# A two-layer hybrid diffusion step on one Trainium2 core: the first latent step opened beside the context top-k, its expert rows spread evenly, w_out by tiles

## The chip, the cores and the metric

The kernel is one program on one core of a Trainium2 chip. The metric is the time of one execution on the device in microseconds; before the change three runs gave a median of 3172.74 us. All data are float32.

## The reference, cut to what matters

There are two layers. In each, a context sequence of 128 tokens and a latent sequence of 256 tokens go through the same weights; the latent one also reads cached context keys and states. D is 1024. PEER retrieves 128 expert rows of U and 128 of V for each token.

```python
def trunk_layer(x, cond, lp, layer_idx, ctx_k, ctx_v, init_f, init_b, latent):
    sh1, sc1, g1, sh2, sc2, g2 = adaln(cond, lp["mod_w"], lp["mod_b"])
    mix, k, v, s_f, s_b = token_mixers(modulate(x, lp["norm1_w"], sh1, sc1), lp, ...)   # w_in, three mixers, w_out
    x = x + g1 * mix
    x = x + g2 * peer_ffn(modulate(x, lp["norm2_w"], sh2, sc2), lp)

def peer_ffn(h, lp):
    q = (xt @ lp["peer_wq"]).reshape(n_tok, 8, 2, 128)
    s = jnp.einsum("thmd,mhnd->thmn", q, lp["peer_keys"])
    v1, i1 = lax.top_k(s[:, :, 0], 16); v2, i2 = lax.top_k(s[:, :, 1], 16)
    top_s, pos = lax.top_k(v1[..., :, None] + v2[..., None, :], 16)      # flattened to 256
    g = jax.nn.softmax(top_s)
    act = jnp.einsum("td,thkd->thk", xb, u_tab[ib])
    return jnp.einsum("thk,thkd->td", jax.nn.gelu(act) * gb, v_tab[ib])
```

## The kernel before

The work is four steps: step 0 is the context of layer 0, step 1 the latent of layer 0, steps 2 and 3 the same of layer 1. A context step has T = 1 tile of 128 tokens, a latent one T = 2. Each step has a dense part (`dense`, one generator for each engine) and a gather, which fetches the picked rows. The gather of a step runs beside the dense part of the next step, and that of step 3 by itself at the end.

**The dense part.** ACT squares x and DVE modulates (`square`, `modulate`, with `inverse_rms` at L1076, a Newton iteration in small VectorE instructions); PE transposes the result (`turn_h`) and multiplies it by w_in in six chunks, q, k, v, xb1, xb0, pz (L606, L616). Then come rope, convolution, the state scan, eight attention heads for a latent step, w_out (L801), transposed keys (L809), the second modulation, the query projection by wq in four chunks (L819), the scores (L831) and, for each tile, `choose`: the top-k on DVE (L1138, L1141, L1146 and what follows), which ends with the mark "picked" (L1246). ACT copies out of PSUM (L889) and takes the softmax exponent in between. The arrays of a step live in regions of one buffer `work`; q and k of a step lie at 0 to 2047, and so do the two one-hot arrays `hot` of the top-k.

**Weights.** SP loads them in chunks of 2 MB into a ring of two (`wring`, `load_chunk` at L359). A chunk is issued when the chunk two before it has been used. SP's order is written out by hand from L456: the chunks, between them the modulation rows (`modulation`, `store_row`, L398, which waits until ACT or DVE has taken the row from PSUM), the modulation vectors, the cached keys, the bands and so on. The last two modulation rows of a layer, 10 and 11, are loaded behind wq of the context step and taken by ACT at its very end.

**The gather.** POOL issues one indirect DMA for each row index of all 128 tokens (L552): 128 partitions of 4 KB, 512 KB. There are 768 such rows of U and 768 of V. They land in a ring of 10 buffers `rows`; from the gather of step 3 on, the 8 halves of `wring` serve too, 18 in all. A buffer is refilled when its row was used, in a fixed order (L547). DVE takes the dot product of a U row with h (L1520), ACT the gelu of 64 of them, DVE multiplies by the gates and spreads the weights of 16 rows (`share`, L1506), and PE accumulates V rows in PSUM in groups of four (L858). When all 128 V rows of a tile are in, DVE adds the sum to x (L1543).

**What sets the order.** Each engine's program is one fixed list. `dense` yields a name at each pause ("start", ("in", 0) ... "mid", ("wq", i), ("ps", t), ("choose", t, i), ("exp", t)), and `run_beside` (L1699) puts there the gather events that the plan has for this name: "u" or "v" (four rows), "g" (gelu), "w" (gates), "s" (share), "x" (sum). `pauses_of` (L1582) gives every pause a weight and `spread` (L1655) hands out the events by weight. `events_one` (L1610) orders the events of a context step's gather in four groups: the first 64 U rows, the first 64 V rows, the other 64 U, the other 64 V, and in `gather_plans` (L1666) each group belongs to one stretch of the latent step: start to dt, ("in", 5) to wo, mid to ("wq", 3), ("ps", 0) to ("exp", 0). `events_two` (L1629) orders those of a latent step's gather evenly: V rows follow 19 groups (LAG) behind U rows. Its first 8 groups of U (EARLY) go beside the second top-k of the step itself, 80% (ROOM) of the rest beside the next context step, and what is left comes after that step (`plan[None]`).

**w_out and what follows.** PE multiplies by w_out column half by column half, both tiles in each half; DVE multiplies by the gate and adds to x (L1483 to L1488); then comes the pause "mid", and after its events DVE modulates (L1490).

## Time and profile before

| | us |
|---|---|
| Median of three runs | 3172.74 |
| Lowest, highest | 3164.27, 3186.46 |
| The profiled execution, its own time | 3179.57 |
| Its span in the profile | 3177.8 |
| Busy in the span: PE, DVE, POOL, ACT | 1557.0, 1617.2, 1734.1, 239.0 |
| First "picked", first row issue | 336.0 |
| Bytes moved by DMA | 981.71 MB |

The windows view gives for stretches of the span the busy time and number of instructions of each engine, TensorE's granted clock as a share of full speed, the busy share of the 16 DMA engines and the rate. POOL's instruction count in a stretch is the number of rows issued. The timeline view gives start and length of instructions, and in brackets how long the engine stood idle before them and what released it. "Issue" is idle time without a releaser.

### The profile page before, as it was taken

Reading aid. Unit: us, or ns where it says so; the run is one execution under the profiler, and the core shown is the slowest. Engines: PE = TensorE matmul, PEld = TensorE weight load, DVE = VectorE, ACT = ScalarE, POOL = GpSimd, SP = SyncE. Lnnn points to the kernel's source line nnn. Section 1 sums busy time; section 2 is a strip of 40 time slices with the busy share of each in tenths; the row PEclk is TensorE's granted clock in tenths of the full one; section 3 lists DMA queues with packets and bytes.
Section 4 is the critical chain, followed back from the end, with each engine's and each line's share of the span. In section 5 each row is a group of like instructions: output and inputs, shape, how many; then the busy total and the mean of one; then the engine's idle time right before and its main releaser. Section 6 shows DMA issues by size and latency. Waiting matters only on the chain.

```text
span 3177.8 us, 22396 instructions
## 1 busy us (share of the span) xinstructions
PE 1557.0 (49%) x6699; PEld 676.8 (21%) x6699; DVE 1617.2 (51%) x4301; ACT 239.0 (8%) x551; POOL 1734.1 (55%) x1540
## 2 busy tenths in 40 slices
PE   6776476756522456645225577666530033332354
PEld 1424253344100132113001144225300000000011
DVE  0124784377397444443861076447639844445411
ACT  0211112111000001000000012110000000000000
POOL 0000663366647655555775673447554867676764
PEclk8888688778666767767557787787765565555576
DMA  6553796778968998999999988678785899999998
GB/s 221 190 193 122 293 399 244 262 259 341 343 204 337 385 342 321 361 368 393 342 331 360 361 326 331 248 263 322 287 331 165 273 376 357 367 368 360 343 361 306
DMA packets 310468, 981.71 MB, mean 309 GB/s; under 512 B 29774, under 2 KB 36212, under 8 KB 310092
## 3 DMA queue, kind: packets, MB, share of 16 engines
q0 software_dynamic: 221184, 805.40, 68.2%
q1 hardware_dynamic: 89164, 174.88, 15.2%
q8 instruction: 54, 0.88, 0.1%
q14 instruction: 66, 0.54, 0.0%
HBM read 976.93 MB, written 3.24 MB: 308 GB/s over the span
## 4 chain that ended last, share of the span: by engine, by line
DVE 23%; PE 22%; issue 18%; DMA 17%; POOL 13%; another core or an unknown queue 5%; ACT 2%; SPq 0%; POOLq 0%; DVEq 0%; ACTq 0%
POOL rows L552 10%; DMA rows<-peer_v_in,vidx 8%; PE acc L858 8%; DVE rows L1520 7%; DMA rows<-peer_u_in,idx 4%; PE psum L574 4%; POOL wring L552 3%; PE psum L801 3%; PE psum L819 2%; DVE work L1141 2%; DVE work L1138 1%; DVE wring L1520 1%; DMA wring<-peer_v_in,vidx 1%; DVE work L1344 1%
## 5 line engine op out<-in xcount | busy, mean ns | idle before, releaser
L552 POOL DMA_INDIRECT rows<-peer_u_in,idx x650 | 793.5, 1221 | 731.2 <-DVE gates L1244 335.6
L1520 DVE CUSTOM_DVE_ANT_0 rows<-rows,hn 128x1024 f32<-128x1024 f32 x650 | 780.0, 1224 | 462.2 <-DMA rows<-peer_u_in,idx 425.1
L552 POOL DMA_INDIRECT rows<-peer_v_in,vidx x654 | 689.6, 1054 | 576.2 <-PE acc L858 349.1
L858 PE MATMUL acc<-rows,vw 128*32 128x512 f32 x2616 | 535.4, 910 | 869.8 <-DMA rows<-peer_v_in,vidx 758.1
L858 PEld LDWEIGHTS acc<-rows,vw 128*32 128x32 f32 x2616 | 107.4, 144 | 1225.1 <-issue 1185.6
L574 PE MATMUL psum<-wring,cond 128*2 128x512 f32 x384 | 186.1, 641 | 112.4 <-DMA wring<-mod_w_in 112.4
L858 PE MATMUL acc<-wring,vw 128*32 128x512 f32 x456 | 128.6, 988 | 192.1 <-DMA wring<-peer_v_in,vidx 92.1
L606 PE MATMUL psum<-wring,work 128*128 128x512 f32 (+1 forms) x480 | 193.0, 559 | 19.6 <-DMA wring<-w_in_in 10.0
L1520 DVE CUSTOM_DVE_ANT_0 wring<-wring,hn 128x1024 f32<-128x1024 f32 x118 | 142.0, 1223 | 113.5 <-DMA wring<-peer_u_in,idx 105.3
L819 PE MATMUL psum<-work,wring 128*128 128x128 f32 (+1 forms) x1024 | 182.1, 342 | 20.1 <-DMA wring<-peer_wq_in 17.4
L889 ACT ACTIVATE work<-psum 128x512 f32<-128x512 f32 (+3 forms) x256 | 110.9, 451 | 908.2 <-PE psum L606 183.7
L552 POOL DMA_INDIRECT wring<-peer_u_in,idx x118 | 136.3, 1155 | 67.8 <-issue 34.4
L819 PEld LDWEIGHTS psum<-work,wring 128*128 128x128 f32 x1024 | 163.2, 201 | 42.5 <-issue 22.9
L552 POOL DMA_INDIRECT wring<-peer_v_in,vidx x114 | 114.5, 1004 | 49.2 <-issue 32.0
L1506 DVE TENSOR_TENSOR vw<-const,wv 128x512 f32<-128x512 f32 x48 | 33.0, 690 | 206.0 <-PE acc L858 140.3
L606 PEld LDWEIGHTS psum<-wring,work 128*128 128x128 f32 x480 | 90.2, 207 | 124.1 <-issue 108.3
L594 PE MATMUL psum<-const,hn 128*128 128x128 f32 x96 | 22.7, 415 | 144.0 <-DVE hn L1132 140.4
L1543 DVE TENSOR_TENSOR acc<-acc,mod_g 128x512 f32<-128x512 f32 x12 | 7.8, 692 | 166.9 <-PE acc L858 121.8
L574 PEld LDWEIGHTS psum<-wring,cond 128*2 128x2 f32 x384 | 33.0, 90 | 258.5 <-issue 255.0
L801 PE MATMUL psum<-wring,work 128*128 128x512 f32 x192 | 86.7, 613 | 0.8 <-ACT work L1025 0.8
L616 PE MATMUL psum<-work,wring 128*128 128x128 f32 (+1 forms) x384 | 76.8, 368 | 16.1 <-DMA wring<-w_in_in 16.1
L858 PEld LDWEIGHTS acc<-wring,vw 128*32 128x32 f32 x456 | 24.8, 152 | 274.2 <-issue 244.9
(203 smaller groups left out, 1394.2 us busy)
## 6 DMA issues: line engine op xcount, KB each, us to landing
wring<-mod_w_in SPq DMA_DIRECT2D x24, 2048.0 KB
wring<-w_in_in SPq DMA_DIRECT2D x20, 2048.0 KB
wring<-peer_wq_in SPq DMA_DIRECT2D x16, 2048.0 KB
wring<-w_out_in SPq DMA_DIRECT2D x8, 2048.0 KB
rows<-peer_v_in,vidx POOLq DMA_INDIRECT x654
rows<-peer_u_in,idx POOLq DMA_INDIRECT x650
wring<-w_in_in SPq DMA_DIRECT2D x4, 1056.0 KB
mod_a<-mod_scratch SPq DMA_DIRECT2D x8, 512.0 KB
```

The source lines that it names most:

```text
L552: nc.gpsimd.indirect_dma_start(slots[slot_of[n]], None, table, bass.IndirectOffsetOnAxis(ap=at[:, col + r:col + r + 1], axis=0))\
L574: mm(p[0:2, :], cond3[:, b, :], w[:, b, :], start=(b == 0), stop=False)
L606: ins = mm(p[:, 0:n], hT[0][:, b, t * P:(t + 1) * P], w[:, b, slot:slot + n], start=(b == 0), stop=(b == DB - 1))
L616: ins = mm(p[:, 0:st.N], w[:, b, i * P:(i + 1) * P], hT[0][:, b, 0:st.N], start=(b == 0), stop=(b == DB - 1))
L801: ins = mm(p[:, :], catT[:, b, t * P:(t + 1) * P], chunk("wo", k, cc)[:, b, :], start=(b == 0), stop=(b == DB - 1))
L819: ins = mm(p[:, 0:N], chunk("wq", k, b // 4)[:, kb, (b % 4) * P:(b % 4 + 1) * P], hT[1][:, kb, 0:N], start=(kb == 0), stop=(kb == DB - 1))
L858: ins = mm(acc[half][QUAD * j:QUAD * (j + 1), :], w[:, at:at + QUAD], four[j][0][:, half * CHUNK:(half + 1) * CHUNK], start=(r == 0), stop ...
L889: A(dst, src, ACT.Copy, scale=scale).then_inc(*take(*key))
L1138: d(V.max(top[:, b * TOPK + 8 * r:b * TOPK + 8 * r + 8], values[:, b * width:(b + 1) * width]))
L1141: d(V.max_index(index[:, b * TOPK + 8 * r:b * TOPK + 8 * r + 8], top[:, b * TOPK + 8 * r:b * TOPK + 8 * r + 8], values[:, b * width:(b + 1 ...
L1506: V.tensor_tensor(vw[q % 2][:, :].rearrange("p (g t) -> p g t", t=QUAD), c("quad").unsqueeze(1).broadcast_to(wide), wv[:, q * SHARE:(q + 1 ...
L1520: V.tensor_tensor_reduce(held, held, hn[n][:, :], 1.0, 0.0, ALU.mult, ALU.add, dots[:, col + r:col + r + 1]).then_inc(u_used, 1)
```

## The change

- The first part of `dense` becomes a generator `opening`: the first square and modulation, the transposes and the q and k projections. For step 1 alone (`early`) it runs inside step 0, at the pauses that `BEFORE` names: after ("wq", 1), ("wq", 2) and ("ps", 0). Its two chunks are loaded behind step 0's wq and ahead of modulation rows 10 and 11. `hot` of the context steps moves to 4096 to 8191.
- The gather of step 0, beside step 1, is ordered by `events_two` and spread over the whole step from ("in", 2) to ("exp", 1). In step 3 the four groups stay, but the last is spread to ("exp", 1).
- PE multiplies by w_out tile by tile; "mid" becomes one pause for each tile, and each tile is squared and modulated ahead of its pause. The transposes of all tiles but the last come ahead of those of the keys. The weights of the pauses change.
- `inverse_rms` does three iterations of two instructions (three for four columns) and one scaling, where it did four of three (four).
- The rows left over after step 2 get 12 more buffers in `work`, those after step 3 get 17. POOL waits for the last "picked" of the step before the first of them. A row takes the free buffer that was used longest ago.
- SP loads the cached keys and values behind pz and waits for the "picked" of the step before.
- In `events_one` the share event stands one place later.

```diff
-        hot = [region(0, 2048), region(2048, 2048)]
+        hot = {False: [region(0, 2048), region(2048, 2048)], True: [region(4096, 2048), region(6144, 2048)]}
...
-            chunks += [(("q", k), ("q", k, last)), (("k", k), ("k", k, last)), (("v", k), ("v", k, last)),
+            if not st.early:
+                chunks += [(("q", k), ("q", k, last)), (("k", k), ("k", k, last))]
+            chunks += [(("v", k), ("v", k, last)),
                        (("xb1", k), ("xb", k, 5)), (("xb0", k), ("xb", k, 3)), (("pz", k), ("pz", k, last))]
             if st.first:
...
+            if k + 1 < STEPS and steps[k + 1].early:
+                chunks += [((name, k + 1), (name, k + 1, steps[k + 1].T - 1)) for name in "qk"]
...
+        left_free = [region(2560 + i * D, D) for i in range(12)]
+        spare(left_free, after_step[STEPS - 2], row_no["u", STEPS - 2, 0, 0])
+        spare([wring[i][:, j * D:(j + 1) * D] for i in range(W_SLOTS) for j in range(DB * CHUNK // D)],
+              row_no["u", STEPS - 1, 0, 0], len(stream))
+        spare([region(i * D, D) for i in range(17)], after_step[STEPS - 1], len(stream))
+        slot_of, held_before, filled, last_in = [], {}, {}, {}
+        for n in range(len(stream)):
+            free = list(range(RING)) + [i for which, first, last in extra if first <= n < last for i in which]
+            slot = min(free, key=lambda i: last_in.get(i, -1))
+            slot_of.append(slot)
             held_before[n] = last_in.get(slot)
             last_in[slot] = n
             filled[n] = filled.get(held_before[n], 0) + 1
+
+        left_by = {after_step[STEPS - 2]: ("picked", STEPS - 2, 0),
+                   after_step[STEPS - 1]: ("picked", STEPS - 1, 1)}
...
+                if st.lat:
+
+                    sp.wait_ge(*after("picked", k - 1, steps[k - 1].T - 1))
+                    sp.wait_ge(*after("h1", k, st.T - 1))
+                    load(k_cached, io["cache_attn_k"][0, layer].rearrange("n h d -> n (h d)"), "cache_in", layer)
+                    load(v_cached, io["cache_attn_v"][0, layer].rearrange("n h d -> n (h d)"), "cache_in", layer)
...
+                if k + 1 < STEPS and steps[k + 1].early:
+                    load_chunk("q", k + 1)
+                    load_chunk("k", k + 1)
...
+                if n in left_by:
+                    pool.wait_ge(*after(*left_by[n]))
...
-                for cc in range(2):
-                    pe.wait_ge(*chunk_landed("wo", k, cc))
-                    for t in range(T):
+                for t in range(T):
+                    for cc in range(2):
+                        pe.wait_ge(*chunk_landed("wo", k, cc))
                         p = job(pe, "wo", k, t, cc)
                         for b in range(DB):
                             ins = mm(p[:, :], catT[:, b, t * P:(t + 1) * P], chunk("wo", k, cc)[:, b, :],
                                      start=(b == 0), stop=(b == DB - 1))
                         ins.then_inc(*made("wo", k, t, cc))
+                    yield ("mid", t)
+                for t in range(T - 1):
+                    turn_h(st, 1, t)
                 pe.wait_ge(*after("keys_in", k))
                 for i in range(4):
                     p = job(pe, "kt", k, i)
...
                         b = 4 * i + j
                         ins = tr(p[:, j * P:(j + 1) * P], keys_nat[:, b * P:(b + 1) * P], ident)
                     ins.then_inc(*made("kt", k, i))
-                yield "mid"
-                turn_h(st, 1)
+                turn_h(st, 1, T - 1)
...
-                for _ in range(4):
+
+                scale = 1.0
+                for _ in range(3):
                     if w == 1:
                         d(V.scalar_tensor_tensor(by, out, mean, out, ALU.mult, ALU.mult))
                     else:
...
                         settle()
                         d(V.tensor_tensor(by, by, mean, ALU.mult))
                     settle()
-                    d(V.tensor_scalar(by, by, -0.5, 1.5, ALU.mult, ALU.add))
-                    settle()
-                    d(V.tensor_tensor(out, out, by, ALU.mult))
-                    settle()
+                    d(V.scalar_tensor_tensor(out, by, 3.0 * scale * scale, out, ALU.subtract, ALU.mult))
+                    settle()
+                    scale *= -2.0 * scale * scale
+                d(V.tensor_scalar(out, out, 1.0 / scale, None, ALU.mult))
...
+            def opening(st):
+                yield "start"
+                modulate(st, 0)
+                yield "h"
+                yield ("in", 0)
+                yield ("in", 1)
...
-                for cc in range(2):
-                    for t in range(T):
-                        tmp = mixed if (cc * T + t) % 2 == 0 else xw
+                for t in range(T):
+                    for cc in range(2):
+                        tmp = mixed if cc == 0 else xw
...
-                yield "mid"
-                modulate(st, 1)
+                    modulate(st, 1, t)
+                    yield ("mid", t)
...
-    names += [("start", 0)]
-    names += [(("in", i), w * T) for i, w in enumerate((15, 7, 7))]
-    names += [("rope", 0)]
+    if not st.early:
+        names += [("start", 0), ("h", 5 * T)]
+        names += [(("in", i), w * T) for i, w in enumerate((10, 7))]
+    names += [(("in", 2), 7 * T), ("rope", 0)]
     names += [(("in", i), w * T) for i, w in ((3, 4.5), (4, 7))]
     names += [("dt", 4), (("in", 5), 7 * T), ("conv", 7), ("xw", 9)]
     for t in range(T):
         names += [(("decay", t), 3), (("seg", t), 14)]
     names += [("y", 3)]
     names += [(("head", i), 6) for i in range(T * ATT_HEADS)]
-    names += [("wo", 9), ("mid", 15 * T)]
-    names += [(("wq", i), (15 if i == 0 else 7) * T) for i in range(4)]
+    names += [("wo", 9)]
+    names += [(("mid", t), 14 if t == 0 else 10) for t in range(T)]
+    names += [(("wq", i), (10 if i == 0 else 7) * T) for i in range(4)]
...
-            groups = left
-            spread(plan, part("start", "dt"), groups[0])
-            spread(plan, part(("in", 5), "wo"), groups[1])
-            spread(plan, part("mid", ("wq", 3)), groups[2])
-            spread(plan, part(("ps", 0), ("exp", 0)), groups[3])
+            if steps[k].early:
+
+                spread(plan, part(("in", 2), ("exp", 1)), left)
+            else:
+                groups = left
+                spread(plan, part("start", "dt"), groups[0])
+                spread(plan, part(("in", 5), "wo"), groups[1])
+                spread(plan, part(("mid", 0), ("wq", 3)), groups[2])
+                spread(plan, part(("ps", 0), ("exp", 1)), groups[3])
...
-            left = events_one(steps[k])
+            left = events_two(steps[k]) if steps[k + 1].early else events_one(steps[k])
...
+BEFORE = {("wq", 1): ("start",), ("wq", 2): ("h",), ("ps", 0): (("in", 0), ("in", 1))}
...
+    def work(st):
+        following = steps[st.k + 1] if st.k + 1 < len(steps) else None
+        ahead = opening(following) if following and following.early else None
+        if st.first:
+            for name in modulation(st.layer):
+                if st.k:
+                    yield name
+        if not st.early:
+            yield from opening(st)
+        for name in dense(st):
+            yield name
+            for expected in BEFORE.get(name, ()) if ahead else ():
+                assert next(ahead) == expected
+        if ahead:
+            assert next(ahead, None) is None
```

## Rows read from the trace of the kernel before

**Rows 1.** The page: busy shares and slices of the span.
```profile
PE 1557.0 (49%) x6699; PEld 676.8 (21%) x6699; DVE 1617.2 (51%) x4301; ACT 239.0 (8%) x551; POOL 1734.1 (55%) x1540
...
DMA  6553796778968998999999988678785899999998
```

**Rows 2.** Windows by stage: from:to, length, each engine's busy us, PE's clock, DMA share, GB/s.
```profile
282.50:336.00 53.50, 15.33 (x36) 2.55 (x33) 50.09 (x246) 1.05 (x3) 0.00 (x0) 0.68 0.05 18
336.00:460.00 124.00, 90.78 (x272) 52.71 (x272) 95.96 (x177) 13.30 (x27) 95.45 (x72) 0.83 1.01 391
460.00:610.00 150.00, 89.05 (x499) 45.89 (x499) 70.98 (x230) 36.13 (x92) 56.17 (x59) 0.75 0.74 270
610.00:686.00 76.00, 38.26 (x129) 18.13 (x128) 41.34 (x87) 6.87 (x13) 36.27 (x29) 0.72 0.71 249
686.00:766.00 80.00, 65.94 (x313) 57.49 (x314) 52.86 (x96) 10.54 (x24) 66.90 (x44) 0.93 0.95 354
766.00:881.00 115.00, 57.71 (x280) 13.22 (x280) 60.16 (x275) 3.10 (x6) 64.86 (x65) 0.69 0.87 316
881.00:968.00 87.00, 9.62 (x22) 1.44 (x20) 85.14 (x298) 0.31 (x1) 42.65 (x30) 0.57 0.55 177
1515.00:1640.00 125.00, 29.22 (x132) 5.66 (x136) 97.44 (x315) 0.42 (x1) 92.69 (x79) 0.56 0.94 341
1650.00:1835.00 185.00, 94.27 (x444) 20.29 (x444) 30.57 (x79) 5.91 (x10) 109.70 (x112) 0.71 0.95 351
2099.00:2246.00 147.00, 98.72 (x383) 72.83 (x380) 93.19 (x177) 15.23 (x33) 92.42 (x71) 0.81 0.86 312
2246.00:2462.00 216.00, 56.00 (x296) 14.48 (x294) 145.11 (x584) 6.40 (x10) 109.58 (x98) 0.59 0.69 246
2462.00:2502.00 40.00, 0.00 (x0) 0.00 (x0) 38.55 (x67) 0.00 (x0) 33.90 (x21) 0.50 0.79 256
2541.00:3165.00 624.00, 224.35 (x1020) 46.61 (x1024) 241.38 (x440) 0.77 (x3) 430.26 (x427) 0.60 0.95 361
2550.00:2575.00 25.00, 7.43 (x36) 1.53 (x40) 10.84 (x19) 0.00 (x0) 18.98 (x20) 0.64 1.03 411
```

**Rows 3.** POOL's waits in step 1, 336 to 968 us: total, times, longest.
```profile
POOL rows L552 <- PE acc L858: 108.1, 19, 32.1
...
POOL rows L552 <- DVE dots L1520: 73.3, 9, 22.3
```

**Rows 4.** POOL's waits in the last gather, 2541 to 3165 us.
```profile
POOL rows L552 <- remote: 38.3, 13, 4.9
...
POOL rows L552 <- DVE dots L1520: 5.9, 1, 5.9
```

**Rows 5.** Timeline of SP's queue at the start of step 1.
```profile
338.33 1.49 SPq L372 DMA_DIRECT2D wring<-w_in_in  x2
```

**Rows 6.** Timeline of PE in step 1: start, length, what, idle before it.
```profile
358.87 29.99 PE L606 MATMUL psum<-wring,work 128*128 128x512 f32 x64 [7.59 <-issue]
394.49 19.00 PE L606 MATMUL psum<-wring,work 128*128 128x512 f32 x64 [5.63 <-DMA wring<-w_in_in]
...
614.85 27.73 PE L801 MATMUL psum<-wring,work 128*128 128x512 f32 x64
...
678.18 1.97 PE L594 MATMUL psum<-const,hn 128*128 128x128 f32 x8 [33.85 <-DVE hn L1132]
```

**Rows 7.** Timeline of DVE: steps 0, 1 and 3, three gaps.
```profile
282.79 3.19 DVE L1138 MAX8 work<-work 128x8 f32<-128x128 f32 x16 [41.77 <-ACT work L889]
...
875.09 1.30 DVE L1543 TENSOR_TENSOR acc<-acc,mod_g 128x512 f32<-128x512 f32 x2 [31.42 <-PE acc L858]
...
2369.80 1.30 DVE L1543 TENSOR_TENSOR acc<-acc,mod_g 128x512 f32<-128x512 f32 x2 [45.10 <-remote]
```

**Rows 8.** The page: costliest groups, busy and mean ns of one.
```profile
L1520 DVE CUSTOM_DVE_ANT_0 rows<-rows,hn 128x1024 f32<-128x1024 f32 x650 | 780.0, 1224 | 462.2 <-DMA rows<-peer_u_in,idx 425.1
```

**Rows 9.** One line of the inverse root: duration ns min, median, max.
```profile
L1095 DVE TENSOR_SCALAR root<-root x108: 153/154/286, 49.0 to 3173.0; 128x1 f32<-128x1 f32 x84, 128x4 f32<-128x4 f32 x24
```

More of the change, by code:

```diff
@@ L861, in gather @@
                             ins.then_inc(v_used, 1)
-            run_beside(steps, plans, lambda layer: modulation(layer, MOD_ORDER[:4]), dense, gather)
+            run_beside(steps, plans, lambda layer: modulation(layer, MOD_ORDER[:4]), opening, dense, gather)
         @block.scalar
@@ L889, in carry, with square @@
                 A(dst, src, ACT.Copy, scale=scale).then_inc(*take(*key))
-            def square(st, which):
-                for t in range(st.T):
+            def square(st, which, only=None):
+                for t in range(st.T) if only is None else (only,):
                     if which == 0:
@@ L1059, in _ @@
             A(cond[:, :], bank("cond")[:, 0:16], ACT.Silu).then_inc(*take("cond"))
-            run_beside(steps, plans, modulation, dense, gather)
+            run_beside(steps, plans, modulation, opening, dense, gather)
         @block.vector
@@ L1567, in _ @@
             dve.wait_ge(*after("consts_in"))
-            run_beside(steps, plans, modulation, dense, gather)
+            run_beside(steps, plans, modulation, opening, dense, gather)
     assert sorted(map(str, took)) == sorted(map(str, numbers)), "each psum job is taken once"
@@ L1620, in events_one @@
         for n, v in enumerate(vs):
[L1621 removed]
+            if n % share == 3 and share < n < lot - share:
                 line.append(("s", k, 0, first + n // share + 1))
@@ L1708, in run_beside @@
         if k < len(steps):
[L1709 removed]
             seen = []
[L1711 to L1716 removed]
+            for name in work(steps[k]):
                 seen.append(name)
                 beside(name)
[L1719 removed]
+            assert seen == [n for n, _ in pauses_of(steps[k])], seen
         beside(None)
```

95 lines of the change are left out of this document (47 added, 48 removed).

## The prediction

> **What bounds the kernel now.** I read the page's shares and slices first, then the windows by stage, then POOL's waits, then single gaps of PE and DVE. No engine is full over the span: PE 49%, DVE 51%, POOL 55%, while the slices of DMA stand at 8 or 9 in most places and dip to 6 or less in a few [rows 1]. Below, "step 0" to "step 3" are context and latent of layer 0, then of layer 1; the rows gathered by POOL (1536 of 512 KB, 805 MB) are most of the traffic. Undisturbed, POOL issues 20 rows in 25 us, 1.25 us each, at 411 GB/s [rows 2]. Against this the stages differ. Step 1 lasts from 336 to 968 us (632 us), and only its first 124 us run at 391 GB/s; then come 270, 249, 354, 316 and 177 GB/s [rows 2]. In this step POOL stood 108.1 us for a buffer that PE had not freed and 73.3 us for one that DVE had not [rows 3]: 181 us of 632. So step 1 is bound by the ring of 10 buffers: its consumers sit in a fixed order behind dense work. The same holds of step 3 (312 GB/s in 2099 to 2246, 246 in 2246 to 2462). The last gather, 2541 to 3165, is different: 361 GB/s, DMA share 0.95, and POOL waits there 38.3 us for a remote party but only 5.9 us for DVE [rows 2, 4]. That stage is bound by transfer. Beside step 0's top-k (282.5 to 336) DMA is idle, share 0.05 [rows 2]. That is where the opening goes.
>
> **The opening of step 1 beside step 0's top-k.** Before, after the pick at 336: w_in's q and k chunks are issued at 338.33 [rows 5], PE multiplies both from 358.87 for 29.99 us, then waits 5.63 us for v, which starts at 394.49 [rows 6]. Afterwards v and xb1 stand in the place of q and k. I expect their issue at 338 as before, since SP still waits at the store of modulation row 10, which ACT takes behind the top-k. So v starts near 359, not 394.5: 35 us off the start of step 1, whose section to 460 becomes 89 us instead of 124. It then holds 10 of the 32 U groups (40 rows) where 72 were issued [rows 2]. Cost in step 0: DVE's two modulations, behind whose wait for mod_a the whole top-k is queued, lie in its 41.77 us gap before it [rows 7]; mod_a is issued between the wq chunks, as now. PE's 30 us of q and k start behind the scores, with 53.5 us to hide in, and ACT's eight copies with them. The two 2 MB chunks take idle DMA. If this cover failed, the pick would come up to 35 us later and nothing were won. Upper bound of the loss: 35; taken: 0.
>
> **U and V evenly through step 1.** The new plan has 77 events over weights of 397, from v's projection to the last piece of the second top-k. I count per section:
> - 460 to 610 (convolution, scan, heads): 13 groups of U and 3 of V, before 59 rows issued, nearly all V. DVE gets 52 rows at 1.224 us [rows 8], 64 us more on top of 71 busy of 150 [rows 2]; PE loses some ten groups of V, 3.5 us each (224.35 us for 1020 matmuls in the last gather, 16 to a group of four rows [rows 2]). Ends: +64 if every U row lies on the chain, -35 if only the V rows did. DVE waits in this part for others in more than half of the time, so I take +14, giving 164.
> - 610 to 686 (w_out to the turned h2): below, 42 instead of 76.
> - 686 to 766 (queries): PE is busy 66 of 80 [rows 2] and gets five V groups more, 18 us, while U rows go; +3 taken (0 to +18), giving 83.
> - 766 to 968 (two top-k): before 65 + 30 issues in 202 us [rows 2], with DVE standing 31.42 us for the last V before tile 0's sum [rows 7]. Now 40 rows in the first top-k and 48 + 32 in the second: 120. The nearest row is step 2's top-k, where U and V already alternate: 79 issues in 125 us, 1.58 us each [rows 2]. 120 x 1.58 = 190, so -12. Ends: 1.31 us, a row at 400 GB/s (157), and 2.9 us (348).
> Sum: 89 + 164 + 42 + 83 + 190 = 568 against 632, **-64 us**.
>
> **w_out by tiles, and "mid".** Before, PE sits idle 33.85 us for h2 behind the keys [rows 6], since DVE takes five U groups between x_mid and the modulation. Now each tile is modulated straight after its x_mid and U follows. w_out (27.73 us [rows 6]), one modulation (15 small instructions of 0.2 us and two passes about as long as a U row, 5 us), and some 9 for transposes and copies make 42 for the 76 us: -34 in step 1, counted above. In step 3 it is the same gap, but behind it the wq chunks and 44 rows load. 2099 to 2246 took 147 us for 71 rows and 8 MB at 312 GB/s [rows 2]; at 390 it would be 118. I take 122: **-25** (-10 to -34).
>
> **The two top-k of step 3.** The old plan spends all 64 V rows of tile 0's second lot up to "exp 0", and DVE stands 45.10 us before the sum [rows 7]; in 2246 to 2462 it is busy 145 of 216 [rows 2]. The new plan stretches them to "exp 1". 64 V + 32 U = 96 rows at 1.58 are 152 us; DVE's 145 plus small waits is the longer: 166. **-50** (-15 to -60).
>
> **The rest.** inverse_rms loses 5 instructions of 15, about 0.2 us each [rows 9], on 27 calls: 27 us of DVE, of which I count 4 in step 0, where nothing covers it, and 5 in step 2 with its reordered square; elsewhere it is inside the sections. The reordered keys cost nothing: PE transposes them while DVE modulates, as now. SP's new wait for the earlier pick holds the cached keys, and behind them the band, the states and w_out, but that pick is done at 336 and the loads come after pz, still ahead of their users: 0 (to +5). The share event moved from 2 to 3 belongs to a plan that step 0's rows no longer use: 0 to 2.
> Late slots: 12 more buffers for the rows left over after step 2 (1650 to 1835, 112 issues, 351 GB/s, share 0.95 [rows 2]) are worth at most the missing 5% plus the hand-over; against them stands POOL's new wait for the pick, which all later issues queue behind. **-5** (-20 to +10). 17 more in the last gather free POOL from 5.9 us of DVE [rows 4], not from the remote waits. But POOL now waits there for the second pick. Before it had run 18 rows ahead, worth 18 x 1.28 = 23 us (512 KB at 411 GB/s), of which part was lost again, since after the pick DVE's rows back to back held POOL to 21 issues in 40 us [rows 2]. **+10** (-15 to +23).
>
> **Sum**: -4 - 64 - 5 - 5 - 25 - 50 + 10 = -143. The profiled execution took 3179.6 us (span 3177.8), so 3036.6; it lay 7 above the median of 3172.7, so **3030 us**. A change under 1% could not be told from none.
>
> **The rivals.**
> (a) *POOL is held by DVE.* In 2462 to 2502 DVE is busy 38.55 of 40 and POOL needs 33.90 / 21 = 1.61 us an issue instead of 0.95, 1.90 with the gap [rows 2]. If the top-k does this to rows too, step 1's 120 cost 228 (+38) and step 3's 96 cost 182 (+16): **3084**. Against it: 1.58 in step 2. The Trainium skill (SBUF — State Buffer, "Who interferes with whom") has it that a VectorE instruction with two SBUF inputs contends only with GpSimd's reads, and that descriptor writing should not suffer. The U rows have two SBUF inputs, and the trace disagrees: 1.61 against 0.95 us.
> (b) *The top-k runs at the free pace.* If most of its instructions leave POOL alone and the slots are enough, 120 rows cost 1.31 us, 157: 33 less, and the tail's +10 becomes -10: **2977**. For it: DVE's busy work there is only 145 us. Against it: no top-k in the trace ran so. By the same section, an instruction with one SBUF input leaves GpSimd alone, which would favour this rival.
> (c) *The top-k stretches stay as they are*, because PE's V groups and DVE's shares wait for each other whatever the order: only the other gains, 81 us, remain: **3092**.
> (d) *Slower.* With V rows for two top-k in one ring of 10, U rows of the new tile queue behind V rows whose weights DVE makes only between its pieces, and the 881 to 968 pace (30 rows in 87 us, 2.9 us) holds for all 216 rows of the four top-k: 626 us against 418. +208 - 81 gives **3300**. It decides from (418 + 81) / 216 = 2.31 us per row. For it: that is the pace of the stage that mixes the two now. Against it: there DVE had 52 us of top-k and all of 32 U rows, and few rows were planned.
> That the opening doesn't leave step 1 would show as 3065 and is part of (a)'s neighbourhood.
>
> **How the numbers follow.** Forecast 0.58, (a) 0.15, (c) 0.12, (b) 0.09, (d) 0.06. The range takes in (b), (a) and (c) with their slack: 2970 to 3115; outside are (d) and the far edges. Slower by over 1% is (d), 0.06; within 1% (3141 to 3204) are the worst of (a) and (c) together, 0.06; faster 0.88.
>
> **What would show it.** First U issue still at 334 to 338 and v's product at about 359. Step 1 over near 900 to 905, its POOL waits under 120 us, PE's gap before h2 under 10 us. DVE's wait before the sum in step 3 gone or under 10. The last gather as long as before or slightly longer. The forecast is wrong if the first pick moves, if the sections 460 to 610 grow beyond 190 us, or if rows in the top-k cost over 2 us.

## The result, and the profile after

The changed kernel takes 3072.23 us (3069.44 to 3083.75, four runs) against 3170.34 us for the kernel before (four runs as well): a ratio of 0.969 with a 95% interval of 0.9646 to 0.9734, 3.1% faster. The profiled execution took 3070.95 us, span 3069.2, so 108.6 us less than the one of before. The forecast was 3030 with a range of 2970 to 3115: right in kind and within the range, too large in the gain (143 us against 108.6 in the profiled executions and 98.1 in the medians).

The page of the changed kernel: DMA's slices stand at 8 or 9 from the ninth to the 25th, where the old page had a 6 in the twelfth, step 1's second top-k [rows 1]. They still dip in the seventh and eighth slice, the scan and heads of step 1, and in most from the 26th to the 31st, in step 3.

```profile
PE 1617.9 (53%) x6699; PEld 688.4 (22%) x6699; DVE 1595.5 (52%) x4160; ACT 240.0 (8%) x552; POOL 1724.9 (56%) x1540
...
DMA  6555796699999999999899989669697999999997
```

For a comparison by stages I cut both spans at the same five kinds of instruction: the gates of a step's last pick, the first matmul of w_out, the first of the queries, the first MAX8 of the top-k, and DVE's sum. The windows of the changed kernel (columns as in [rows 2]):

```profile
332.00:593.70 261.70, 129.25 (x528) 79.73 (x528) 185.86 (x414) 44.83 (x109) 150.22 (x114) 0.70 0.80 292
593.70:633.40 39.70, 36.22 (x133) 16.64 (x129) 20.44 (x43) 6.31 (x12) 21.76 (x20) 0.97 0.81 292
633.40:718.00 84.60, 75.68 (x377) 58.10 (x378) 28.62 (x49) 8.65 (x21) 39.45 (x39) 0.90 0.94 356
718.00:904.20 186.20, 80.87 (x374) 17.86 (x373) 145.74 (x575) 5.39 (x9) 129.75 (x117) 0.61 0.93 333
904.20:1628.60 724.40, 337.12 (x1471) 127.51 (x1470) 389.98 (x929) 49.16 (x114) 453.61 (x388) 0.70 0.95 353
1628.60:1772.20 143.60, 88.42 (x396) 19.31 (x394) 6.66 (x22) 2.58 (x5) 92.36 (x98) 0.76 0.99 387
1772.20:2040.50 268.30, 186.49 (x801) 102.07 (x801) 163.96 (x378) 49.70 (x117) 143.26 (x125) 0.81 0.82 305
2040.50:2082.20 41.70, 33.08 (x101) 16.45 (x97) 25.77 (x53) 6.42 (x12) 18.38 (x16) 0.89 0.76 283
2082.20:2177.70 95.50, 67.48 (x297) 58.53 (x298) 65.16 (x108) 10.17 (x23) 69.20 (x56) 0.82 0.97 371
2177.70:2347.20 169.50, 56.51 (x282) 13.12 (x280) 139.98 (x568) 5.15 (x8) 97.96 (x86) 0.58 0.76 267
2347.20:3058.40 711.20, 271.24 (x1024) 59.21 (x1024) 313.85 (x578) 1.02 (x4) 508.74 (x480) 0.60 0.94 356
```

Set beside the kernel before, cut the same way:

| Stage | before | after | difference | forecast |
|---|---|---|---|---|
| up to step 0's pick | 334.8 | 332.0 | -2.7 | -4 |
| step 1: pick to w_out | 280.1 | 261.7 | -18.4 | -21 |
| step 1: w_out to queries | 71.5 | 39.7 | -31.8 | -34 |
| step 1: queries to top-k | 80.5 | 84.6 | +4.1 | +3 |
| step 1: two top-k | 194.6 | 186.2 | -8.4 | -12 |
| step 2 | 714.5 | 724.4 | +9.9 | -5 |
| left-over rows of step 2 | 148.6 | 143.6 | -5.0 | -5 |
| step 3: to w_out | 274.5 | 268.3 | -6.2 | 0 |
| step 3: w_out to top-k | 148.8 | 137.2 | -11.6 | -25 |
| step 3: two top-k | 214.4 | 169.5 | -44.9 | -50 |
| the last gather | 703.7 | 711.2 | +7.5 | +10 |

The opening: PE multiplies by q and k from 281.94, beside the top-k; SP issues the next chunks at 335.60, behind the stores of the modulation rows; v starts at 356.44, and PE has stood 30.30 us for it. First PE's timeline, then SP's, of the changed kernel:

```profile
281.94 27.73 PE L638 MATMUL psum<-wring,work 128*128 128x512 f32 x64 [0.90 <-ACT work L927]
...
356.44 19.04 PE L638 MATMUL psum<-wring,work 128*128 128x512 f32 x64 [30.30 <-DMA wring<-w_in_in]
```

```profile
332.09 2.14 SPq L426 DMA_DIRECT2D mod_scratch<-mod_rows  x2
...
335.60 47.28 SPq L397 DMA_DIRECT2D wring<-w_in_in  x4
```

The wait before a tile's sum is gone. In step 3 DVE goes from the last U row straight to the gates and the sum, where [rows 7] had 45.10 us (timeline of DVE, changed kernel):

```profile
2345.46 1.22 DVE L1572 CUSTOM_DVE_ANT_0 rows<-rows,hn 128x1024 f32<-128x1024 f32 x1
...
2347.16 0.29 DVE L1292 TENSOR_TENSOR gates<-work,small 128x128 f32<-128x128 f32 x1
2347.49 1.30 DVE L1595 TENSOR_TENSOR acc<-acc,mod_g 128x512 f32<-128x512 f32 x2
```

POOL's waits in step 1 fell from 181 us [rows 3] to 148, which is more than the 120 that the prediction gave as a sign of being right:

```profile
POOL rows L584 <- PE acc L896: 92.5, 21, 13.7
...
POOL rows L584 <- DVE dots L1572: 55.5, 10, 19.3
```

### The profile page after: what moved, and what is told of

It reads as the page before. It is cut to its first block, busy times and chain, and to the rows that moved or that the text cites. A ratio compares the mean times of both kernels' runs of the same rounds, so it can differ in the third digit from the quotient of the medians.

```text
span 3069.2 us, 22265 instructions
## 1 busy us (share of the span) xinstructions
PE 1617.9 (53%) x6699; PEld 688.4 (22%) x6699; DVE 1595.5 (52%) x4160; ACT 240.0 (8%) x552; POOL 1724.9 (56%) x1540
## 4 chain that ended last, share of the span: by engine, by line
PE 28%; issue 20%; DVE 19%; DMA 17%; POOL 11%; another core or an unknown queue 3%; ACT 2%; SPq 0%; POOLq 0%; DVEq 0%; ACTq 0%
PE acc L896 10%; DVE rows L1572 6%; POOL rows L584 5%; DMA rows<-peer_v_in,vidx 5%; DMA rows<-peer_u_in,idx 5%; POOL work L584 4%; PE psum L857 4%; PE psum L606 4%; DMA wring<-w_in_in 3%; PE psum L638 2%; PE psum L837 2%; POOL wring L584 2%; DMA work<-peer_v_in,vidx 2%; DVE work L1189 1%
## 5 line engine op out<-in xcount | busy, mean ns | idle before, releaser
L584 POOL DMA_INDIRECT rows<-peer_u_in,idx x591 | 710.3, 1202 | 651.0 <-DVE gates L1292 332.8
L1572 DVE CUSTOM_DVE_ANT_0 rows<-rows,hn 128x1024 f32<-128x1024 f32 x591 | 708.2, 1224 | 436.3 <-DMA rows<-peer_u_in,idx 410.2
L584 POOL DMA_INDIRECT rows<-peer_v_in,vidx x519 | 567.0, 1092 | 485.1 <-PE acc L896 306.1
L896 PE MATMUL acc<-rows,vw 128*32 128x512 f32 x2076 | 434.0, 901 | 592.1 <-DMA rows<-peer_v_in,vidx 454.0
L896 PE MATMUL acc<-work,vw 128*32 128x512 f32 x720 | 216.8, 855 | 331.5 <-DMA work<-peer_v_in,vidx 179.5
L584 POOL DMA_INDIRECT work<-peer_v_in,vidx x180 | 183.5, 1019 | 92.4 <-issue 50.1
L857 PE MATMUL psum<-work,wring 128*128 128x128 f32 (+1 forms) x1024 | 183.6, 343 | 11.6 <-DMA wring<-peer_wq_in 8.6
L1572 DVE CUSTOM_DVE_ANT_0 work<-work,hn 128x1024 f32<-128x1024 f32 x110 | 133.1, 1224 | 102.7 <-DMA work<-peer_u_in,idx 84.6
L584 POOL DMA_INDIRECT work<-peer_u_in,idx x110 | 120.9, 1099 | 48.3 <-issue 32.9
L584 POOL DMA_INDIRECT wring<-peer_u_in,idx x67 | 69.6, 1039 | 23.8 <-issue 22.0
```

Source lines behind the costliest of these rows:

```text
L584: nc.gpsimd.indirect_dma_start(slots[slot_of[n]], None, table, bass.IndirectOffsetOnAxis(ap=at[:, col + r:col + r + 1], axis=0))\
L857: ins = mm(p[:, 0:N], chunk("wq", k, b // 4)[:, kb, (b % 4) * P:(b % 4 + 1) * P], hT[1][:, kb, 0:N], start=(kb == 0), stop=(kb == DB - 1))
L896: ins = mm(acc[half][QUAD * j:QUAD * (j + 1), :], w[:, at:at + QUAD], four[j][0][:, half * CHUNK:(half + 1) * CHUNK], start=(r == 0), stop ...
L1572: V.tensor_tensor_reduce(held, held, hn[n][:, :], 1.0, 0.0, ALU.mult, ALU.add, dots[:, col + r:col + r + 1]).then_inc(u_used, 1)
```

## The experiments

Three sets were run, each on a chip of its own and with the kernel before beside it. The kernel before took 3156.82, 3055.34 and 3173.49 us in them, so times of different sets aren't compared; ratios to the kernel before are. The bases are 0.969 (with the result) and 0.9696 (set 2). From the two intervals, a difference between two ratios is known to 0.5 or 0.6%, 15 to 19 us.

Stages differ between the sets as well. In set 1 the kernel with "exp 0" in step 3 has the same step 1 as the changed kernel, and its step 1 takes 580.6 us, not the 572.2 of the profile with the result. It is the base for step 1 in that set. Its four stretches (pick to w_out, to the queries, to the top-k, to the pick):

```profile
333.00:601.70 268.70, 134.56 (x529) 83.17 (x529) 185.50 (x413) 44.77 (x109) 150.62 (x114) 0.68 0.79 285
601.70:641.30 39.60, 36.15 (x132) 16.60 (x128) 20.41 (x43) 6.30 (x12) 21.72 (x20) 0.97 0.82 292
641.30:726.00 84.70, 75.68 (x377) 58.09 (x378) 28.64 (x49) 8.67 (x21) 39.78 (x39) 0.90 0.94 356
726.00:913.60 187.60, 79.13 (x377) 18.07 (x376) 145.53 (x576) 5.35 (x9) 129.65 (x117) 0.66 0.92 331
```

### Set 1: one part taken out

**The opening put back.**

```diff
-                self.early = k == 1
+                self.early = False
+                self.even = k == 1
...
-            if steps[k].early:
-
-                spread(plan, part(("in", 2), ("exp", 1)), left)
+            if steps[k].even:
+
+                spread(plan, part("start", ("exp", 1)), left)
```

> The changed kernel with the opening of step 1 put back at the start of step 1; its rows still alternate, now spread from "start" to the second "exp". My theory (each stage bound by the ring pays for itself): the pick of step 0 stays at 332 to 335 us, step 1 grows by 25 to 35 us, and the whole is 3095 to 3107. Rival (the rows only move, and transfer gives the time back later): at most 10 us more, 3072 to 3082.

Measured: 3086.46 us, ratio 0.9794 (0.9753 to 0.9835), so 1.0% above the base, 33 us. Step 1 takes 594.9 us, 14.3 more than in the base of its set (22.7 more than with the result):

```profile
335.00:627.20 292.20, 168.49 (x640) 97.60 (x640) 205.81 (x453) 50.28 (x120) 167.58 (x130) 0.73 0.82 305
627.20:666.90 39.70, 36.21 (x133) 16.70 (x129) 16.60 (x36) 6.30 (x12) 12.07 (x12) 0.97 0.76 265
666.90:763.70 96.80, 75.59 (x361) 58.09 (x362) 27.56 (x47) 10.04 (x23) 49.07 (x44) 0.85 0.88 320
763.70:929.90 166.20, 71.30 (x358) 16.77 (x357) 140.75 (x568) 3.88 (x7) 112.51 (x103) 0.67 0.91 325
```

Up to w_out it is 23.5 us longer than in its set's base and up to the top-k 12 more, but the two top-k take 166.2 instead of 187.6, with 14 fewer rows left for them. With the even order the opening pays; part of it is given back. The rival (at most 10 us) is out by the ratio, if narrowly. Where the rest of the 33 us lies isn't shown: the profiled execution was one of the two quickest of this kernel (3079.9 us).

**The four groups kept.**

```diff
-            if steps[k].early:
-
-                spread(plan, part(("in", 2), ("exp", 1)), left)
-            else:
+            if True:
                 groups = left
-                spread(plan, part("start", "dt"), groups[0])
+                spread(plan, part(("in", 2) if steps[k].early else "start", "dt"), groups[0])
...
-            left = events_two(steps[k]) if steps[k + 1].early else events_one(steps[k])
+            left = events_one(steps[k])
```

> The changed kernel with the early opening, but step 0's rows in the four old groups (64 U, 64 V, 64 U, 64 V) over the stretches in 2 to dt, in 5 to wo, mid to wq 3, ps 0 to exp 1. My theory: the first stretch becomes bound by transfer (64 rows and four chunks in some 90 us) and eats most of what the opening saves, so 20 to 35 us more, 3092 to 3107. Rival (the order doesn't matter once the last group reaches exp 1): within 8 us of 3072.

Measured: 3072.82 us, ratio 0.9733 (0.9678 to 0.9788), 0.4% above the base, within what can be told. Step 1 takes 572.9 us: as long as with the result, and 7.7 less than in the base of its set.

```profile
333.90:425.00 91.10, 59.64 (x192) 38.65 (x192) 62.60 (x101) 4.53 (x12) 69.76 (x51) 0.75 0.98 369
333.90:609.90 276.00, 155.79 (x720) 87.00 (x720) 153.57 (x352) 43.13 (x108) 153.90 (x131) 0.72 0.83 308
609.90:651.60 41.70, 32.76 (x100) 16.29 (x96) 25.74 (x53) 6.42 (x12) 18.46 (x17) 0.92 0.77 281
651.60:748.00 96.40, 66.60 (x311) 57.79 (x312) 65.09 (x108) 9.71 (x23) 79.64 (x56) 0.84 0.99 373
748.00:906.80 158.80, 59.04 (x276) 13.45 (x276) 140.24 (x568) 3.89 (x7) 101.99 (x88) 0.61 0.84 301
```

The first part of the mechanism is as I expected: the first stretch is full at 369 GB/s, w_out comes 7 us later than in the set's base, and the queries take 12 us more. But I priced it wrongly: the top-k, with 88 rows instead of 117, gives back 29 us. My forecast of 20 to 35 us fell, and the rival's "within 8 us" holds of step 1 in the profiles.

**Step 3's last group to exp 0 again.**

```diff
-                spread(plan, part(("ps", 0), ("exp", 1)), groups[3])
+                spread(plan, part(("ps", 0), ("exp", 0)), groups[3])
```

> The changed kernel, but in step 3 the last 64 V rows and the sum end at exp 0 again, as before the change. My theory: DVE's wait of about 45 us before the sum comes back, the two top-k of step 3 take 205 to 215 us instead of 169.5, and the whole is 3105 to 3117. Rival (rows moved out of the stretch are found again in the last gather): 3075 to 3090.

Measured: 3110.81 us, ratio 0.9865 (0.9822 to 0.9908), 1.75% or some 55 us above the base; in the profiles 32.5 us of span, of two sets. DVE waits again (timeline), and the two top-k take 203.7 us:

```profile
2288.98 1.30 DVE L1595 TENSOR_TENSOR acc<-acc,mod_g 128x512 f32<-128x512 f32 x2 [34.47 <-remote]
```

```profile
2179.80:2383.50 203.70, 53.78 (x269) 12.55 (x268) 142.86 (x571) 5.12 (x8) 91.29 (x86) 0.58 0.63 229
```

It is the same 86 rows and about the same busy time of DVE (143 us) as in 169.5 us; the other three kernels of this set, with "exp 1", take 165.6 to 167.4. What a better order of this stretch saves is not given back later: the last gather takes 707.4 us here and 706 to 712 in those three.

**The old order of w_out and mid** (the shown core is DVE's; PE and ACT likewise).

```diff
-                for t in range(T):
-                    for cc in range(2):
-                        tmp = mixed if cc == 0 else xw
+                for cc in range(2):
+                    for t in range(T):
+                        tmp = mixed if (cc * T + t) % 2 == 0 else xw
...
-                    modulate(st, 1, t)
-                    yield ("mid", t)
+                for t in range(T):
+                    yield ("mid", t)
+                modulate(st, 1)
```

> The changed kernel with w_out by column halves for both tiles, the keys ahead of both transposes, and U rows ahead of both modulations again. My theory: w_out to the queries takes 70 us instead of 40 in steps 1 and 3; in step 1 this is paid in full, in step 3 by 12 us, together 3105 to 3117. Rival (the queries are bound by transfer in both steps and take back what is lost): 3080 to 3092.

Measured: 3101.45 us, ratio 0.9831 (0.98 to 0.9862), 1.4% above the base; 25.5 us of span. W_out to the queries takes 58.8 and 60.9 us instead of 39.7 and 41.7 (not 70, most likely because the new weights give "mid" fewer rows: 24 are issued where it was 29). In step 3 the queries then take 83.9 us instead of 95.5 with the result, or 93 to 94 in this set:

```profile
601.50:660.30 58.80, 39.67 (x133) 18.53 (x129) 26.15 (x52) 6.52 (x12) 25.16 (x24) 0.79 0.79 284
660.30:743.40 83.10, 74.07 (x377) 57.00 (x378) 22.77 (x39) 8.64 (x21) 33.82 (x36) 0.91 0.80 300
2066.10:2127.00 60.90, 33.40 (x101) 17.01 (x97) 35.12 (x69) 6.52 (x12) 31.85 (x24) 0.76 0.76 259
2127.00:2210.90 83.90, 69.53 (x311) 60.05 (x312) 55.34 (x92) 9.83 (x23) 64.69 (x49) 0.87 0.98 370
```

In step 3, where the queries run at 370 GB/s, 19 us saved ahead of them cost 9 to 12 in them. In step 1 they run at 300 here and give next to nothing back (83.1 us against 84.7); over the whole of step 1 13.5 us are left.

### Set 2: late buffers, v earlier, the even order in step 3

**The base.**

> The changed kernel itself, as the base for its neighbours on this chip: ratio to the kernel before 0.965 to 0.973 as measured with the result.

Measured: 2965.59 us, ratio 0.9696 (0.966 to 0.9732).

**Without the late buffers.**

```diff
-        spare(left_free, after_step[STEPS - 2], row_no["u", STEPS - 2, 0, 0])
...
-        spare([region(i * D, D) for i in range(17)], after_step[STEPS - 1], len(stream))
...
-                if n in left_by:
-                    pool.wait_ge(*after(*left_by[n]))
```

> The changed kernel without the 12 and the 17 late buffers and without POOL's two new waits for the pick (the 8 buffers in wring stay). My theory: the 12 are worth about 5 us between step 2's pick and the last sum of its left-over rows, the wait before the last gather costs about as much, so within 10 us of the changed kernel either way. Rival (the deeper ring carries the gain): 20 to 40 us slower.

Measured: 2971.8 us, ratio 0.973 (0.9694 to 0.9766), 6 us beside the base and not to be told from it. The left-over rows take 144.8 instead of 140.0 us, as sized, and the last gather 646.6 instead of 649.3, so that of the +10 for POOL's wait no more than 3 are seen here. The rival is out.

**v and xb1 ahead of the stores.**

```diff
                              .broadcast_to([2, CHUNK]), "nw_in", layer, j)
+                    if j == order[-1]:
+                        for key in ahead:
+                            load_chunk(*key)
                     if j != order[0]:
                         store_row(*before)
...
-                    modulation(layer, MOD_ORDER[10:])
+                    modulation(layer, MOD_ORDER[10:], [("v", k + 1), ("xb1", k + 1)] if steps[k + 1].early else ())
```

> The changed kernel with the v and xb1 chunks of step 1 issued ahead of the stores of modulation rows 10 and 11, so beside step 0's top-k. In the profile of the changed kernel PE stands 30.3 us for v at the start of step 1. My theory: v is multiplied before the pick, the convolution starts 20 to 25 us earlier, and 8 to 20 us remain at the end of step 1, since DMA is then the bound of the first stretch: 0.3 to 0.6% faster than the changed kernel. Rival (the stretch is bound by DVE's and the ring's order): no gain, within 5 us.

Measured: 2947.33 us, ratio 0.9627 (0.9579 to 0.9674), 18 us or 0.6% under the base of its set. Its four runs took 2933.95 to 2959.38 us, those of the base 2959.12 to 2969.12, but the intervals of the two ratios overlap: faster than the changed kernel in all likelihood. The product of v starts at 329.2, before the pick at 335.0 (timeline of PE):

```profile
329.20 17.47 PE L642 MATMUL psum<-wring,work 128*128 128x512 f32 x64
346.52 7.15 PE L652 MATMUL psum<-work,wring 128*128 128x256 f32 x32
362.48 15.68 PE L652 MATMUL psum<-work,wring 128*128 128x256 f32 x64 [8.80 <-DMA wring<-w_in_in]
```

The pick to w_out takes 247.8 instead of 264.6 us. Of these 17 us, 12 are left at the end of step 1, which takes 559.2 us against 571.5 (571.1 and 568.9 in the two other kernels of this set, whose step 1 is that of the base).

**The even order beside step 3 too.**

```diff
-            else:
-                groups = left
-                spread(plan, part("start", "dt"), groups[0])
-                spread(plan, part(("in", 5), "wo"), groups[1])
-                spread(plan, part(("mid", 0), ("wq", 3)), groups[2])
-                spread(plan, part(("ps", 0), ("exp", 1)), groups[3])
+            spread(plan, part(("in", 2) if steps[k].early else "start", ("exp", 1)), left)
...
-            left = events_two(steps[k]) if steps[k + 1].early else events_one(steps[k])
+            left = events_two(steps[k])
```

> The changed kernel with step 2's rows alternating evenly over the whole of step 3 as well, from start to the second exp. My theory: the scan and heads of step 3 take more rows (125 issues now in 268 us), the queries fewer, and POOL's waits of 72.7 us for PE before w_out halve; step 3 gets 10 to 30 us shorter, 3045 to 3063 where the changed kernel takes 3072. Rival (the order within the step is nothing, as the pair with four groups in step 1 suggests): within 8 us.

Measured: 3007.36 us, ratio 0.9835 (0.9796 to 0.9874), 1.4% slower than the base: my theory fell, and the rival too. Step 3 takes 574.1 us instead of 536.3. The stretch up to w_out, of the base and then of this kernel:

```profile
1769.00:2028.40 259.40, 181.29 (x800) 98.20 (x800) 163.58 (x378) 49.94 (x117) 137.66 (x122) 0.81 0.84 317
```

```profile
1765.80:2049.80 284.00, 171.14 (x640) 99.49 (x640) 206.34 (x455) 49.88 (x117) 153.32 (x121) 0.74 0.79 289
```

POOL issues the same number of rows, 122 and 121, but DVE is busy 206 us instead of 164: it takes 106 U rows in this stretch instead of 66, between the small steps of scan and heads. POOL's wait moves from PE (71.5 to 36.6 us) to DVE (18.2 to 55.4 us):

```profile
POOL rows L584 <- DVE dots L1572: 55.4, 5, 16.4
POOL rows L584 <- PE acc L896: 36.6, 4, 11.5
```

### Set 3: what each part gives by itself

**Four iterations** of the old loop in the changed kernel.

```diff
-                for _ in range(3):
+                for _ in range(4):
...
-                    d(V.scalar_tensor_tensor(out, by, 3.0 * scale * scale, out, ALU.subtract, ALU.mult))
+                    d(V.tensor_scalar(by, by, -0.5, 1.5, ALU.mult, ALU.add))
+                    settle()
+                    d(V.tensor_tensor(out, out, by, ALU.mult))
...
-                d(V.tensor_scalar(out, out, 1.0 / scale, None, ALU.mult))
```

> The changed kernel with four iterations of the old form in inverse_rms (135 more small VectorE instructions of 0.2 us). My theory: the calls in step 0, and a few behind SSD and heads, lie on the path; 4 to 12 us slower than the changed kernel, ratio to the kernel before 0.970 to 0.974. Rival (all hidden under transfers): 0.967 to 0.970.

Measured: 3093.46 us, ratio 0.9733 (0.9703 to 0.9764), 0.4% above the base, 13 us, and inside the ratios expected; 22.5 us of span, of two sets. That is no more than the two ratios can differ by chance, and this set has no run of the changed kernel, so neither my 4 to 12 us nor the rival is ruled out.

**Four groups and the early v**, the two edits shown above together.

```diff
+                spread(plan, part(("in", 2) if steps[k].early else "start", "dt"), groups[0])
...
+                        for key in ahead:
+                            load_chunk(*key)
```

> Step 0's rows in the four groups and v and xb1 ahead of the stores. With the even order the early v brought the ratio from 0.9696 to 0.9627. My theory: in the groups the first stretch holds 64 U rows and is bound by transfer, so that nothing of the early v is left, ratio 0.969 to 0.975. Rival (the gain is one of PE's chain, whatever the order): 0.962 to 0.967.

Measured: 3079.77 us, ratio 0.9701 (0.9672 to 0.973). The groups without the early v had 0.9733, and the two intervals overlap. The early v gives 17 us up to w_out in the even order and nothing here: 277.2 us against 276.0. The products of w_in end 58 us after the pick instead of 91, but the first matmul of dt starts 123 us after it instead of 122, as DVE has 60 U rows ahead of the steps that it needs. PE stands idle for 65 us (timeline; in the groups without the early v it is 30.60). The profile names nobody for this wait; in the opening-alone kernel below, where it is 28.75, it names DVE:

```profile
453.15 0.56 PE L689 MATMUL psum<-par,const 128*128 128x4 f32 x2 [65.26 <-issue]
```

In the even order DVE has 28 rows there, and this matmul starts 85 us after the pick, or 64 with the early v.

**Exp 1 alone in the kernel before**, one word of the plan.

```diff
-            spread(plan, part(("ps", 0), ("exp", 0)), groups[3])
+            spread(plan, part(("ps", 0), ("exp", 1)), groups[3])
```

> The kernel before with one word changed: the last 64 V rows and the sum stretch to exp 1 instead of exp 0, in steps 1 and 3. My theory: DVE's waits of 31.4 and 45.1 us before the two sums go, step 3's top-k take 165 to 175 us instead of 214, step 1's about 165 to 175 instead of 195; ratio 0.976 to 0.984, more than half of the whole change. Rival (the gain is in the order and the opening, and this alone gives only what undoing it in step 3 cost, or less): 0.985 to 0.990.

Measured: 3113.39 us, ratio 0.9806 (0.9785 to 0.9827). By itself this word brings 1.94%, where the whole change brings 3.1. The top-k of steps 1 and 3:

```profile
765.50:927.00 161.50, 60.37 (x277) 13.56 (x277) 139.97 (x568) 3.85 (x7) 102.44 (x88) 0.60 0.84 299
...
2222.00:2390.90 168.90, 56.90 (x281) 12.98 (x280) 140.13 (x567) 5.11 (x8) 104.29 (x89) 0.60 0.76 270
```

**The opening alone**: the four groups, the old w_out and mid, loop and buffers as in the edits above, and

```diff
-            left = events_two(steps[k]) if steps[k + 1].early else events_one(steps[k])
+            left = events_one(steps[k])
...
-                spread(plan, part(("ps", 0), ("exp", 1)), groups[3])
+                spread(plan, part(("ps", 0), ("exp", 0)), groups[3])
```

> The changed kernel with everything but the opening put back: four groups to exp 0, old order of w_out and mid, four iterations, no late buffers (the pauses' new weights and the later load of the cached keys stay). My theory: the first stretch of step 1 is bound by transfer when it holds 64 U rows, so the early q and k gain at most 10 us, ratio 0.997 to 1.002. Rival (parts add up; with the even order the opening was worth 22 us of step 1): 0.990 to 0.995.

Measured: 3177.45 us, ratio 1.0007 (0.9988 to 1.0027): nothing. The timeline of PE shows where most of the opening goes. All products of w_in are done at 426, and then PE stands for DVE:

```profile
360.56 19.66 PE L634 MATMUL psum<-wring,work 128*128 128x512 f32 x64 [30.78 <-DMA wring<-w_in_in]
...
411.94 14.00 PE L634 MATMUL psum<-wring,work 128*128 128x512 f32 x32 [0.19 <-DMA wring<-w_in_in]
454.69 0.56 PE L681 MATMUL psum<-par,const 128*128 128x4 f32 x2 [28.75 <-DVE par L1372]
```

DVE has 60 U rows to take before the steps of dt, and they come at the pace of transfer, 383 GB/s up to 460. Of the 35 us saved ahead some 29 are waited for here, and 6 are left at w_out (273.8 us from the pick against 280.1). Step 1 ends up 9.8 us shorter than before, and what it gains is lost behind it: step 2 takes 720.5 us, where the kernel of the same set with "exp 1" alone takes 710.5.

## Why the prediction was right or wrong

**Right: what bounds the kernel.** The stages bound by the ring paid for themselves: undoing exp 1 was not made up for elsewhere, and undoing the new mid only in part. Where a stage was bound by transfer (369 to 383 GB/s), the saving ahead of it was given back, wholly or in part. Of the 34 us by which the sum was too large, 15 are step 2's and 13 those of w_out and the queries of step 3.

**Right: the opening's timing.** I had v near 359 and SP held by the store of row 10; the trace has 356.44 and 335.60. The pick moved by -2.7, so the cover held. My -35 + 14 = -21 for pick to w_out was -18.4.

**Right in size, wrong in what it was credited to: the top-k of step 1.** The 1.58 us per row of [rows 2] was met: 117 rows in 186.2 us, 1.59. But I credited the -12 to the even order. With the groups, and only exp 1, this stretch takes 161.5 us, 33 less than before, and step 1 as a whole 590.1, 37 less. The even order moves 29 rows into this stretch (117 against 88), out of the stretch up to w_out and out of the queries. So 1.59 was no price of a row: with 88 rows it is 1.80 us, and DVE's 140 us of work are the larger part of the stretch. With the even order step 1 takes 572.2 and 580.6 us in two sets, with the groups 572.9, and the ratios differ by 0.4% the other way: which order is better isn't told. The even order is not idle, though: it lets the opening and the early v through, since DVE then has 28 U rows ahead of dt, not 60. But up to w_out it also costs: without the opening it takes 292.2 us, and the groups with exp 1 alone take 280.2. What the opening gives in the even order may thus be little more than what the even order takes; the changed kernel with the groups and without the opening would tell, and wasn't run.

**Right: w_out by tiles in step 1** (-31.8 for -34), **exp 1 in step 3** (-44.9 for -50), the late buffers and the last gather (-5.0 and +7.5 for -5 and +10). In the last term I counted 18 rows issued ahead of the pick, where the trace has 11 (469 of the 480 come after it), and the remote waits of the ring's buffers alone (38.3 us), where over all buffers they are 56.

**Wrong: the term for w_out and the queries of step 3.** I took 122 us for 147 and wrote that at 390 GB/s the bytes would need 118. The stretch took 137.2. Its first part ran at 283 GB/s with only 16 rows issued instead of 28, so that 56 were left for the queries, and these ran at 371. I let the whole stretch go at the free rate, though in the first part POOL waits for a buffer 27 of 42 us, where it was 28 of 71.

**Wrong: step 2**, forecast -5, measured +9.9. By the profiles it takes 714.5 us before, 710.5 with exp 1 alone, 720.5 with the opening alone and the new weights, and 724.4 in the changed kernel. The loss is all ahead of w_out, 425.3 us instead of 413.8 (the kernel before, then the changed one):

```profile
961.50:1375.30 413.80, 204.74 (x774) 72.01 (x774) 208.13 (x463) 34.06 (x81) 251.08 (x215) 0.69 0.95 359
904.20:1329.50 425.30, 215.36 (x815) 70.35 (x813) 212.87 (x459) 34.06 (x81) 266.75 (x226) 0.72 0.98 367
```

This stretch is bound by transfer, and 11 more rows are issued in it. At 367 GB/s a row takes 1.43 us, so they would cost 16 us. After w_out 14 fewer rows are issued, but that part stays as long (300.7 us, then 299.1). With exp 1 alone 218 rows come ahead of w_out, in 412.2 us, and with the opening alone 223, in 419.3. The new weights are smaller for "mid" and the queries, which puts four rows more ahead of w_out in the plan; I had not priced them. That they are the cause is argued from these counts: no run has the changed kernel with the old weights, and where the other seven rows come from is open.

**Not told: inverse_rms.** I counted 9 us on the path of 27 us of work. Taking it back costs 0.4%, 13 us, with an uncertainty that takes in both and nothing.

**The rivals.** (a), rows in the top-k at 1.90 us, is out in step 1 with 1.59, and in step 3 the two top-k take 169.5 us, not 182 (1.97 us for each of 86 rows, but there DVE is busy for 140 of them); (b), the free pace of 1.31, is out too; (c), the top-k unchanged, is out in step 3, and in step 1 the stretch shrank by only 8.4 us because rows were moved into it, not because shares and V rows wait for each other; (d), slower from 2.31 us per row on, was far off.

## What to carry to other kernels

Where a gather and a dense part share fixed instruction orders and a small ring, look first for the one wait that closes a tile, here the sum behind the last V row: moving it by one top-k brought 1.9% by itself, where taking the opening out cost 1.0% and taking the even order out 0.4%, which is not clear of noise. The parts don't add up to the whole: measure a part both alone and taken out. Work opened early pays only if what needs it isn't queued behind rows that come at the pace of transfer; count the rows between them (28 against 60 here). An order that does no harm in one step can hurt in another: with 40 more U rows beside the scan and heads of step 3 that stretch took 25 us more. That DVE's small steps are the chain there is argued, from POOL's waits for DVE.

## What the runs showed of the hardware

In the first part of the last gather of the kernel before, POOL needed 1.61 us for an indirect DMA while DVE ran U rows back to back, against 0.95 us elsewhere [rows 2]; beside the top-k of the changed kernel it was 1.11 us (129.75 us for 117). That is not a matter of U or V rows. In the whole trace of the kernel before, an issue with no DVE instruction beside it takes 0.94 us on average for either (241 and 359 of them). Where DVE's products with U rows cover at least half of it, it takes 1.52 us for a U row and 1.25 for a V row (310 and 196). The Trainium skill (SBUF — State Buffer, "Who interferes with whom") infers that an instruction with two SBUF inputs does not hold up descriptor writing; these numbers do not bear that out for the indirect DMA. It also reads its row indices from SBUF, and no run tells whether the reading or the writing is held up.

In the last gather POOL stood up to 6.6 us at a time for a remote party, with no buffer named by the profile: 56 us before, over all buffers, and 42 us after the change, with 35 buffers instead of 18. On the chip of set 2 it didn't stand so at all, in none of the four kernels. The sets differed more than the change: the kernel before took 3055.34 us on that chip and 3173.49 on the one of set 3. The last gather of the changed kernel took 711.2 us at 356 GB/s with the result and 649.3 us at 391 GB/s in set 2, for the same 480 rows; 42 of these 62 us are the remote waits:

```profile
2305.30:2954.60 649.30, 210.61 (x1024) 41.69 (x1024) 314.37 (x577) 1.02 (x4) 490.18 (x480) 0.59 1.00 391
```
